# Paged sparse attention on Trainium2: the sampling loop taken three batches deep, its pages loaded whole

## The reference

```python
    sub = x.reshape(B, nsub, CMP_STRIDE, N_KV, HEAD_DIM)
    parts = jnp.einsum('bnsgd,ms->bmngd', sub, pool.reshape(r, CMP_STRIDE))
    pooled = parts[:, 0, :nc]
    for m in range(1, r):
        pooled = pooled + parts[:, m, m:m + nc]
    pooled = pooled + jnp.einsum('l,ld->d', pool, pe)
    return jax.nn.gelu(pooled) @ phi
...
        qg = qc.reshape(B, qc_len, N_KV, GROUP, HEAD_DIM)
        s = jnp.einsum('bqgnd,bcgd->bgnqc', qg, k_cmp, preferred_element_type=jnp.float32) * scale
        dist = (pc[:, None] - cmp_end[None, :]).astype(jnp.float32)
        valid = cmp_end[None, :] <= pc[:, None]
        s = s - slopes[:, :, None, None] * dist
        p = jax.nn.softmax(jnp.where(valid, s, NEG), axis=-1) * valid
        o_c = jnp.einsum('bgnqc,bcgd->bqgnd', p.astype(v_cmp.dtype), v_cmp)
        imp = jnp.einsum('bgnqc,cs->bgqs', p, overlap)
        cur = pc // SEL_BLOCK
        forced = (blk_ids[None, :] == 0) | (blk_ids[None, :] == cur[:, None]) | (blk_ids[None, :] == cur[:, None] - 1)
        imp = jnp.where(forced, FORCE_SCORE, imp)
        imp = jnp.where(blk_ids[None, :] <= cur[:, None], imp, -1.0)
        _, idx = lax.top_k(imp, n_top)
        kg = k_blk[bi, gi, idx]
        vg = v_blk[bi, gi, idx]
        kpos = idx[..., None] * SEL_BLOCK + jnp.arange(SEL_BLOCK, dtype=jnp.int32)
        dsel = pc[None, None, :, None, None] - kpos
        s2 = jnp.einsum('bqgnd,bgqksd->bgnqks', qg, kg, preferred_element_type=jnp.float32) * scale
        s2 = s2 - slopes[None, :, :, None, None, None] * dsel[:, :, None].astype(jnp.float32)
        s2 = jnp.where(dsel[:, :, None] >= 0, s2, NEG)
        sh = s2.shape
        p2 = jax.nn.softmax(s2.reshape(*sh[:-2], -1), axis=-1).reshape(sh)
        o_s = jnp.einsum('bgnqks,bgqksd->bqgnd', p2.astype(vg.dtype), vg)
```

## Time and profile before

| | |
|---|---|
| device time, median of 3 runs | 2428.31 us (2425.02, 2428.31, 2799.05) |
| profiled execution, its own time | 2436.58 us |
| its span, first to last instruction | 2434.6 us |
| PE, DVE, ACT, POOL busy over the span | 88%, 45%, 33%, 3% |
| granted TensorE clock, mean | 0.935 of full |
| sampling stage in it | from 755 to 1159.1 us, 404 us |
| its turns 1 to 7 | 43.8 to 51 us each |

### The profile page before, as it was taken

One profiled execution on the slowest core, in us unless ns is written; L12 is line 12 of the kernel. 1 busy time (PEld: TensorE's weight loads), 2 busy tenths in 40 slices (PEclk: granted clock), 3 DMA queues, 4 the chain that ended last, 5 costly groups with the idle time before them and its releaser, 6 DMA issues.

```text
span 2434.6 us, 39677 instructions
## 1 busy us (share of the span) xinstructions
PE 2145.5 (88%) x15836; PEld 1993.7 (82%) x15836; DVE 1083.9 (45%) x1736; ACT 811.1 (33%) x1160; POOL 68.2 (3%) x133
## 2 busy tenths in 40 slices
PE   6999797897896674666699999999999999999997
PEld 5999786776884343444699998999999999999997
DVE  3333476743562233233355544444444444444443
ACT  4222232232342333333443333332333323223344
POOL 1000011000000000000000010000000000000001
PEclk9999898998997777786799999999999999999999
DMA  5644642443335666563655554545544555455443
GB/s 148 186 134 133 144 126 78 126 111 115 111 122 198 220 208 195 162 209 105 241 170 143 151 153 123 155 127 152 165 143 140 157 151 155 132 162 155 143 131 115
DMA packets 571112, 364.90 MB, mean 150 GB/s; under 512 B 66753, under 2 KB 546578, under 8 KB 569906
## 3 DMA queue, kind: packets, MB, share of 16 engines
q1 hardware_dynamic: 489474, 314.14, 43.2%
q10 hardware_dynamic: 80096, 41.25, 6.4%
q0 software_dynamic: 1424, 7.97, 0.8%
HBM read 345.58 MB, written 23.63 MB: 152 GB/s over the span
## 4 chain that ended last, share of the span: by engine, by line
PE 49%; DMA 1%; DVE 1%; ACT 1%; issue 0%; POOLq 0%; POOL 0%; SPq 0%; ACTq 0%; DVEq 0%
PE bank L280 48%; DMA w_raw<-in_w_attn_out_dram 1%; DVE w_lo L259 1%; ACT w_hi L254 0%; PE bank L2070 0%; DVE hx L2209 0%; ACT ysT L2098 0%; DVE rstd L2254 0%; ACT xT L2156 0%; ACT xT L2177 0%; DVE arena L2283 0%; ACT sq L2128 0%; ACT hx L2103 0%; PE bank L2079 0%; ACT oT L2156 0%
## 5 line engine op out<-in xcount | busy, mean ns | idle before, releaser
L280 PE MATMUL bank<-hx,w_hi 128*128 128x320 f32 x3328 | 734.7, 310 | 5.6 <-DVE w_lo L259 5.6
L280 PE MATMUL bank<-actr,w_hi 128*128 128x320 f32 x3072 | 684.9, 312 | 30.0 <-DVE w_lo L259 28.8
L259 DVE TENSOR_TENSOR w_lo<-w_raw,w_hi 128x2048 fp32r<-128x2048 f32 (+2 forms) x222 | 464.1, 2091 | 372.1 <-ACT w_hi L254 372.1
L280 PEld LDWEIGHTS bank<-hx,w_hi 128*128 128x128 f32 x3328 | 558.3, 188 | 6.1 <-DVE w_lo L259 6.1
L280 PEld LDWEIGHTS bank<-actr,w_hi 128*128 128x128 f32 x3072 | 519.8, 190 | 31.9 <-DVE w_lo L259 17.6
L280 PE MATMUL bank<-hx,w_lo 128*128 128x320 f32 x1664 | 515.3, 310 | 0.0
L254 ACT CAST w_hi<-w_raw 128x2048 fp32r<-128x2048 f32 (+2 forms) x222 | 386.4, 1741 | 335.9 <-PE bank L280 321.1
L280 PE MATMUL bank<-actr,w_lo 128*128 128x320 f32 x1536 | 478.0, 311 | 0.0
L280 PEld LDWEIGHTS bank<-hx,w_lo 128*128 128x128 f32 x1664 | 313.4, 188 | 0.0
L280 PEld LDWEIGHTS bank<-actr,w_lo 128*128 128x128 f32 x1536 | 292.0, 190 | 0.0
L655 PE MATMUL bank<-actr,half_hi 128*128 128x320 f32 x1024 | 242.0, 325 | 27.6 <-DVE half_lo L626 27.6
(11 more groups left out here) (379 smaller groups left out, 1756.5 us busy)
## 6 DMA issues: line engine op xcount, KB each, us to landing
arena<-in_cache_kv_dram SPq DMA_DIRECT2D x128, 384.0 KB, 4.1
w_raw<-in_w_gate_dram SPq DMA_DIRECT2D x44, 1024.0 KB, 5.2
w_raw<-in_w_up_dram SPq DMA_DIRECT2D x44, 1024.0 KB, 5.2
w_raw<-in_w_down_dram SPq DMA_DIRECT2D x64, 704.0 KB, 4.6
half_raw<-in_w_in_dram ACTq DMA_DIRECT2D x64, 512.0 KB, 4.2
w_raw<-in_w_in_dram SPq DMA_DIRECT2D x20, 1024.0 KB, 5.1
arena<-in_cache_kv_dram SPq DMA_DIRECT2D x128, 128.0 KB, 2.4
w_raw<-in_w_glu_dram SPq DMA_DIRECT2D x32, 512.0 KB, 4.6
```

Source lines behind the costliest of these rows:

```text
L259: nc.vector.tensor_tensor(w_lo[s][:, 0:job.kt * job.width], raw[s][:, 0:job.kt * job.width], w_hi[s][:, 0:job.kt * job.width].bitcast(F32) ...
L280: mm = pe.matmul(bank[:, 0:NT], w[s][:, at:at + P], x[:, kk, :], start=first and k == 0 and m == 0, stop=final and k == job.kt - 1 and m == 2)
```

## The change

The loop gets a third stage and a batch is back only one turn after its exponentials: in turn t batch t is in front, batch m = t - 1 in the middle, batch k = t - 2 has its probabilities turned (`turn_p`) and multiplied by values (`times_v`), and `last_k` = t - 3 is transposed into `oT`. There are NB + 3 turns.

- **Pages whole.** One load brings all 1024 columns of a page (SP: 16 page loads a batch for 32). There are 16 page slots (`RQ` = 4 quads) for 8. After a quad has landed, POOL copies its values (128x1024) into one of two buffers `Vss`; a slot is loaded again when the pooling of its quad and this copy are done (`v_kept`). From batch 2 on the copy of a quad waits until the products of the batch two before have used the same quad of `Vss`.
- **Window and new rows** have two buffers (`wns`, `vnews`) and are loaded by `load_recent(t)` behind the four quads of batch t + 1.
- **More buffers**: three `Ss`, two `Sws`, two row sums, two `ods`; the value products go to PS[0], the merged rows alternate between PS[1] and PS[2]. The room comes from `actr`, which is released during this stage and taken anew after it.
- **Order.** `back` is cut into six `turn_p` and six `times_v` that stand between the steps of front and middle. The gelu of a batch moves to the start of the next turn, behind the exponentials of the batch in the middle. The mask is added before `keep_pool(f, 3)`.

```diff
+        QP, RQ = 4, 4
+        RP = RQ * QP
         NQUAD = NPG // QP
-        pageA = [take(768) for _ in range(RP)]
-        wn = take_x(4 * 512).rearrange("p (t n) -> p t n", t=4)
-        Vs = take(NPG * 256).rearrange("p (g n) -> p g n", g=NPG)
+        quad = [take(QP * 1024).rearrange("p (j n) -> p j n", j=QP) for _ in range(RQ)]
+        pageA = [quad[n // QP][:, n % QP, :] for n in range(RP)]
+        wns = [take_x(4 * 512).rearrange("p (t n) -> p t n", t=4) for _ in range(2)]
+        vnews = [take_x(2 * 256).rearrange("p (a n) -> p a n", a=2) for _ in range(2)]
+        Vss = [take(NPG * 256).rearrange("p (g n) -> p g n", g=NPG) for _ in range(2)]
...
-        Ss = [take(PAST + NQ) for _ in range(2)]
-        Sw = take(WIN + NQ)
+        Ss = [take(PAST + NQ) for _ in range(3)]
+        Sws = [take(WIN + NQ) for _ in range(2)]
...
                 def load_quad(b, q):
-                    if b or q >= 2:
-                        sp.wait_ge(S("score_full"), SCORE["pool", b - (q < 2), (q - 2) % NQUAD] + 1)
+                    at = b * NQUAD + q
+                    if at >= RQ:
+                        sp.wait_ge(S("score_full"), SCORE["pool", (at - RQ) // NQUAD, (at - RQ) % NQUAD] + 1)
+                        sp.wait_ge(S("v_kept"), at - RQ + 1)
                     for j in range(QP):
-                        n = b * NPG + q * QP + j
-                        sp.dma_start(pageA[n % RP], rows[bass.ds(page(b, q * QP + j), 1), :, 0:768].rearrange("o t n -> (o t) n"))\
+                        n = at * QP + j
+                        sp.dma_start(pageA[n % RP], rows[bass.ds(page(b, q * QP + j), 1), :, :].rearrange("o t n -> (o t) n"))\
                             .then_inc(S(f"page_landed{n % RP}"), 16)
...
-                load_quad(0, 0)
-                load_quad(0, 1)
-                for t in range(NB + 1):
-                    if t:
...
-                            sp.wait_ge(S("pv_used"), 6 * m)
...
-                    for q in range(2, NQUAD + 2):
-                        if t < NB and (q < NQUAD or t + 1 < NB):
-                            load_quad(t + q // NQUAD, q % NQUAD)
-                        if t:
-                            for p in range(4 * (q - 2), 4 * (q - 1)):
-                                sp.dma_start(Vs[:, p, :], rows[bass.ds(page(t - 1, p), 1), :, 768:1024].rearrange("o t n -> (o t) n")).then_inc(S("v_landed"), 16)
...
+                def load_recent(m):
+                    v = m % 2
+                    if m >= 2:
+                        sp.wait_ge(S("pv_used"), 6 * (m - 1))
+                    sp.dma_start(wns[v], state_win[0, m].rearrange("(t p) a g d -> p t (a g d)", p=P)).then_inc(S(f"wn_landed{v}"), 16)
+                    sp.dma_start(vnews[v][0:NQ, 0, :], kvr_sample[0, m, :, 3].rearrange("t g d -> t (g d)")).then_inc(S(f"wn_landed{v}"), 16)
+                    sp.dma_start(vnews[v][0:NQ, 1, :], win_sample[0, m, WIN - NQ:WIN, 1].rearrange("t g d -> t (g d)")).then_inc(S(f"wn_landed{v}"), 16)
...
+                for q in range(RQ):
+                    load_quad(0, q)
+                for t in range(NB):
+                    if t + 1 < NB:
+                        for q in range(NQUAD):
+                            load_quad(t + 1, q)
+                    load_recent(t)
...
+                    for q in range(NQUAD):
+                        at = b * NQUAD + q
+                        if b >= 2:
+                            pool.wait_ge(S("pv_used"), 6 * (b - 2) + q + 1)
+                        for j in range(QP):
+                            n = at * QP + j
+                            pool.wait_ge(S(f"page_landed{n % RP}"), 16 * (n // RP + 1))
+                        nc.gpsimd.tensor_copy(Vss[b % 2][:, q * QP:(q + 1) * QP, :], quad[at % RQ][:, :, 768:1024]).then_inc(S("v_kept"), 1)
...
-                def back(m):
...
+                def turn_p(k, n):
+                    bank = turn_bank("p", k, n)
+                    pe.wait_ge(S("p_ready"), 2 * k + (1 if n < 4 else 2))
+                    if n < 5:
...
+                    tr.then_inc(S("turned"), 1)
+                def times_v(m, k):
+                    pe.wait_ge(S("turn_copied"), TURN["p", m, k] + 1)
+                    if k == 0:
+                        pe.wait_ge(S("v_kept"), NQUAD * (m + 1))
+                        if m:
+                            pe.wait_ge(S("so_done"), m)
+                    for br in ((0,) if k < 4 else (1,) if k == 4 else (0, 1)):
...
+                    mm.then_inc(S("pv_used"), 1)
...
+                for t in range(NB + 3):
+                    f, m, k, last_k = (b if 0 <= b < NB else None for b in (t, t - 1, t - 2, t - 3))
                     if f is not None:
                         turn_and_pool(f, 0)
-                    if t >= 2:
-                        pe.wait_ge(S("od_ready"), t - 1)
-                        nc.tensor.transpose(PS[3][:, P:2 * P], od.rearrange("p u d -> p (u d)"), ident).then_inc(S("odT_full"), 1)
-                    if t > NB:
-                        break
+                    if last_k is not None:
+                        pe.wait_ge(S("od_ready"), last_k + 1)
+                        nc.tensor.transpose(PS[0][:, P:2 * P], ods[last_k % 2].rearrange("p u d -> p (u d)"), ident).then_inc(S("odT_full"), 1)
...
                     if m is not None:
                         pe.wait_ge(S("gelu_ready"), 2 * m + 2)
                         if m:
-                            pe.wait_ge(S("so_done"), m)
+                            pe.wait_ge(S("imp_read"), m)
...
-                        turn_and_pool(f, 1)
...
-                        pe.wait_ge(S("wn_landed"), 48 * (m + 1))
+                    if k is not None:
+                        turn_p(k, 0)
+                    if f is not None:
+                        turn_and_pool(f, 1)
+                    if k is not None:
+                        turn_p(k, 1)
+                        times_v(k, 0)
+                    if m is not None:
+                        pe.wait_ge(S(f"wn_landed{m % 2}"), 48 * (m // 2 + 1))
...
+                    if f is not None:
+                        scores(f, 1)
+                        merge(f, 1)
+                    if m is not None:
+                        pe.wait_ge(S("cp_ready"), m + 1)
+                        nc.tensor.transpose(PS[3][0:NC_S, P:2 * P], Pcs, ident).then_inc(S("pcT_full"), 1)
+                    if k is not None:
+                        turn_p(k, 2)
+                        times_v(k, 1)
...
-                        pe.wait_ge(S("cp_ready"), m + 1)
-                        nc.tensor.transpose(PS[3][0:NC_S, P:2 * P], Pcs, ident).then_inc(S("pcT_full"), 1)
                     if f is not None:
-                        scores(f, 1)
-                        merge(f, 1)
...
+                    if k is not None:
+                        turn_p(k, 3)
+                        times_v(k, 2)
                     if f is not None:
                         scores(f, 2)
                         merge(f, 2)
                     if m is not None:
                         pe.wait_ge(S("imp_copied"), m + 1)
                         pe.matmul(PS[3][:, 384:384 + NBLK], C("same"), imp0, start=True, stop=True).then_inc(S("impsum_full"), 1)
+                    if k is not None:
+                        turn_p(k, 4)
+                        times_v(k, 3)
                     if f is not None:
                         turn_and_pool(f, 3)
+                    if k is not None:
+                        turn_p(k, 5)
+                        times_v(k, 4)
+                    if f is not None:
                         scores(f, 3)
                         merge(f, 3)
-                    if m is not None:
-                        pe.wait_ge(S("imp_read"), m + 1)
-                        back(m)
+                    if k is not None:
+                        times_v(k, 5)
...
+                for t in range(NB + 3):
+                    f, m, k, last_k = (b if 0 <= b < NB else None for b in (t, t - 1, t - 2, t - 3))
+                    if m is not None:
+                        act.wait_ge(S("merged"), NQUAD * (m + 1))
+                        if m:
+                            act.wait_ge(S("cv_full"), m)
+                        for v in range(2):
+                            nc.scalar.activation(plS[:, 2 * v:2 * v + 2, :], PS[1 + m % 2][:, 256 * v:256 * (v + 1)].rearrange("p (a c) -> p a c", a=2),
+                                                 ACT.Gelu_apprx_tanh, bias=pec[:, v:v + 1]).then_inc(S("gelu_ready"), 1)
                     if f is not None:
                         copy_keys(f, 0)
...
+                    if k is not None:
+                        copy_p(k, 0)
                     if f is not None:
                         copy_keys(f, 1)
```

220 lines of the change are left out of this document (103 added, 117 removed).

## The result

The changed kernel takes 2345.22 us (median of 4 runs, 2341.27 to 2347.73); before takes 2426.71 beside it. The ratio on record is 0.964, 95% interval 0.961 to 0.967; the quotient of these two medians is 0.966. A slow run of before (2799.05 us) counts in its median and not in the ratio. Run once more, beside the last experiments, the ratio was 0.963 (0.960 to 0.965), and before's medians beside the experiments are 2431.75 to 2434.14 us. The profiled execution took 2344.96 us, span 2343.2.

A forecast was written before the change was run, and what follows sets the result against it. SP's issuing of 32 loads a batch, 1.12 us each, was taken as the bound. Full turns of 34 for 49.5 us end the stage at 1070.8, 88 us sooner: 2436.6 - 88 = 2348.6, on the median's footing 2340 (range 2316 to 2374).

The forecast's parts named there:

- The bound and the ring: Full turn: SP's issuing stops binding; a ring of DVE, ACT and PE takes 32.4 us, with clock loss 34.
- The ring's DVE and ACT half: From the sum over heads through choice, mask, maxima, exponentials and table load to the gelu's end: 12.95 us.
- The PE half: PE from the gelu to the next sum over heads: 14.4 + 4.1 + 0.9 = 19.4 us, clock loss 2 besides.
- The data path: POOL's copy, SP and landing, then a turn's pages and window at 340 GB/s: 31.4 us, fitting in the turn.
- Turn 1: Batch 0's window lands at 813; 13.6 us of work and 0.5 for a low clock end the turn at 827.
- First turn, last turns, end: Turn 0 ends near 788, turn 8 at 1060.5, turn 9 and the last transpose at 1070.8.
- From the stage to the whole: Stage loses 88 us, other stages 0: profiled 2436.6 becomes 2348.6, or 2340 on the median's footing, 8 lower.
- Rival 1: Transfers bind at 236 GB/s: turns of 43.6 us, 2422 in all; chance 0.05.
- rival 2: PE's clock stays at 1.2 GHz throughout: turns of 51.8 us, 2455 in all; chance 0.03.
- Rival 3: POOL's copies over 3.7 us or unfound in-order waits: turns of 38 to 41 us, 2364 to 2382; chance 0.15.
- Rival 4: The products still wait for something of the same turn, so the change doesn't do what it says; under 1%.

The follow-up runs named there:

- filled_wait: Changed kernel with 7 and 18 spare transposes on PE ahead of its waits at L1721 and L1728: 2331.51 us, ratio 0.958.
- window0_first: Changed kernel with batch 0's window and new rows loaded ahead of batch 1's pages: 2331.50 us, ratio 0.959.
- after_again: The changed kernel itself, unedited, run once more beside the last experiments: 2337.30 us, ratio 0.963.
- gelu_first: Changed kernel with each batch's gelu moved ahead of the exponentials of the batch before: 2315.19 us, ratio 0.952.
- reordered: Changed kernel with gelu and first key copies ahead of exponentials, windows earlier, POOL's fourth copy behind the mask, output's turn behind the first merge: 2296.26 us, ratio 0.945.

## Why the prediction was right, step by step

**The bound and the ring: right.** The 17 us wait went, PE waits for the gelu at L1728, and SP's issuing doesn't bind. Turns of 34 were forecast and 33.96 measured. The ring's DVE and ACT half was put at 12.95 and took 13.43, of which 0.59 is the slowed L1984, the one thing that the rows of before could not show. The PE half was put at 19.4 and 2 for the clock; it took 20.5, of which the clock is 1.57 (filled_wait), so 19.0 and 1.57. The two waits were 4.0 us a turn (2.93 and 1.08), forecast 4.6 in one.

**The data path: right in the verdict, too slow in size.** I took 340 GB/s at full share from the earlier trace rows; whole pages came at 414 to 423 at full share. POOL's copy took 1.04 us, put at 1.1. From the end of the first product's wait (copy at 910.29) the window had landed by 938, 28 us on, put at 31.4, and it was needed at 944.

**Turn 1: right by two errors that cancel.** The window landed at 807.2, not 813 (the rate again). But behind the 11 us wait PE worked at 0.50 for 8.8 us, where I had put 0.5 for a low clock. window0_first gives the price: from the window's turning to the sum over heads it takes 8.8 us at full clock (796.88 to 805.70), after 13.0 (807.18 to 820.14), 4.1 more. Turn 2's L1728 was thus due at 827 + 6.8 = 833.8 and came at 832.94.

**First turn, last turns, end.** Turn 0 ended at 788.3 (788), though it started 1.7 us late; the probabilities of batch 7 were first used at 1058.68 (1060.5), the stage ended at 1068.5 (1070.8).

**From the stage to the whole: the step that was off.** The profiled executions differ by 91.6 us (88 forecast), the medians by 81.5. I had assumed that after's profiled execution would lie 8 us above its median as before's did. It lay at its median, so the median came out at 2345, 5 over the forecast of 2340. Nor was the 8 us firm: it came from three runs, and beside the experiments before's medians lie only 2 to 5 us under its profiled 2436.58. Such an offset belongs to an execution, not to a kernel: SP started the stage at 756.77 in after and at 748.72 in after_again, the same program, and the profiles' spans are 10.3 us apart. What in the stages ahead makes this difference was not looked into.

**The rivals.** Rival 1 (transfers bind) is excluded by gelu_first and reordered, which move the same bytes in 30.2 and 28.5 us. Of rival 2 (low clock) 1.57 us a turn is true, far from what it needed. (The prediction lets it decide from a turn of 48.6 us on, without a derivation; its own sum, 830 + six turns + 45, meets before's end at 1159.1 with turns of 47.4.) Rival 3's in-order waits and slow copies did not come. Rival 4 is excluded by the waits.

## What to carry to other kernels

When a change removes a long wait, follow the ring once more with the new order, engine by engine, and ask of each table load, copy and turn behind the last result whether it could stand ahead of it: here such moves were worth another 2%, two thirds of it by putting the gelu ahead of the exponentials. Price the idle time that stays at more than its length: here 4 us of it in a turn cost 1.6 us more through the clock, and 11 us cost 4.1. And try the two parts of a change apart: each alone only met the other's wait, so neither alone shows what the pair is worth.
